# Starting the inverse of the delta stage from 8x8 diagonal blocks solved on VectorE

## What is computed

```
lmat = where(strict, einsum("nbhid,nbhjd->nbhij", kb, kc) * decay, 0.0)
amat = eye + lmat
tinv = triangular_solve(amat, eye, left_side=True, lower=True, unit_diagonal=True)
u = tinv @ (vc * bc[..., None])
w = tinv @ (kb * jnp.exp(gc)[..., None])
```

## Time and profile before

| | |
|---|---|
| median of 3 runs | 877.53 us (875.87 to 878.43) |
| profiled execution | 872.16 us, span 870.3 us |
| mean granted TensorE clock | 0.976 |
| TensorE busy (matmul) | 786.0 us, 90% |
| VectorE, ScalarE, GpSimd busy | 318.2, 169.7, 16.1 us |
| HBM read | 288.30 MB, 334 GB/s over the span |

### The profile page before, as it was taken

The page is one execution under the profiler, slowest core; times in us unless marked ns, Lnnn a source line. Parts: engine busy times, 40 slices in busy tenths (PEclk is TensorE's granted clock), DMA queues, the critical chain, the costliest instruction groups (busy, mean ns, idle before and its releaser), DMA issues.

```text
span 870.3 us, 16568 instructions
## 1 busy us (share of the span) xinstructions
PE 786.0 (90%) x7235; PEld 528.1 (61%) x7235; DVE 318.2 (37%) x662; ACT 169.7 (20%) x327; POOL 16.1 (2%) x21
## 2 busy tenths in 40 slices
PE   4999998989998999999967878999899999988776
PEld 3788667678798655456533443679865556644334
DVE  1154545722523533443322240132453443341324
ACT  3112412213223211111100141040311111110013
POOL 0000000011100000000000000000000000000000
PEclk9999999999999999999989999999999999997899
DMA  9999679383799499999999999993569999999991
GB/s 342 386 358 344 230 236 350 136 306 107 252 390 364 162 393 364 379 414 418 415 416 412 403 386 385 390 411 140 194 233 389 354 396 415 416 418 416 410 398 71
DMA packets 93274, 291.52 MB, mean 335 GB/s; under 512 B 11321, under 2 KB 14479, under 8 KB 78863
## 3 DMA queue, kind: packets, MB, share of 16 engines
q1 hardware_dynamic: 82352, 284.31, 84.2%
q10 hardware_dynamic: 10847, 6.11, 2.4%
HBM read 288.30 MB, written 2.10 MB: 334 GB/s over the span
## 4 chain that ended last, share of the span: by engine, by line
PE 74%; DMA 11%; SPq 9%; DVE 3%; ACT 2%; issue 2%; ACTq 1%; DVEq 0%
PE psum L1322 14%; PE psum L1312 7%; PE psum L1246 7%; PE psum L897 6%; PE psum L1367 6%; DMA scratch<-in_w_exp_up 5%; PE psum L957 5%; PE psum L850 4%; PE psum L1378 4%; PE psum L1488 3%; PE psum L1019 3%; PE psum L1500 3%; SPq L734 3%; DMA ring<-in_w_exp_up 2%; DMA scratch<-in_w_in_odd 2%
## 5 line engine op out<-in xcount | busy, mean ns | idle before, releaser
L1322 PE MATMUL psum<-scratch,hT 128*32 128x512 f32 (+2 forms) x512 | 121.4, 642 | 15.1 <-DMA scratch<-in_w_exp_up 15.1
L1322 PE MATMUL psum<-ring,hT 128*32 128x512 f32 (+1 forms) x416 | 88.2, 621 | 10.8 <-DMA scratch<-in_w_exp_up 10.8
L1312 PE MATMUL psum<-scratch 128*128 128x128 f32 x704 | 82.4, 275 | 0.9 <-DVE scratch L2392 0.9
L1312 PEld LDWEIGHTS psum<-scratch 128*128 128x128 f32 x704 | 80.3, 192 | 1.2 <-issue 1.2
L1322 PEld LDWEIGHTS psum<-scratch,hT 128*32 128x32 f32 (+2 forms) x512 | 35.5, 131 | 64.1 <-issue 64.0
L1322 PEld LDWEIGHTS psum<-ring,hT 128*32 128x32 f32 (+1 forms) x416 | 24.4, 120 | 62.6 <-issue 62.6
L1378 PEld LDWEIGHTS psum<-const,scratch 128*128 128x128 bf16 x480 | 45.1, 97 | 23.8 <-issue 13.6
L897 PE MATMUL psum<-hT,ring 128*128 128x256 f32 x256 | 57.8, 382 | 1.1 <-DVE hT L2012 0.7
L1378 PE MATMUL psum<-const,scratch 128*128 128x256 bf16 x480 | 55.9, 272 | 3.0 <-DVE scratch L2408 3.0
L1246 PE MATMUL psum<-hT,ring 128*128 128x128 f32 x512 | 58.1, 275 | 0.3 <-issue 0.3
L1246 PEld LDWEIGHTS psum<-hT,ring 128*128 128x128 f32 x512 | 57.6, 192 | 0.9 <-issue 0.8
(11 more groups left out here) (316 smaller groups left out, 913.4 us busy)
## 6 DMA issues: line engine op xcount, KB each, us to landing
ring<-in_w_mod SPq DMA_DIRECT2D x42, 1024.0 KB, 8.9
scratch<-in_w_exp_down SPq DMA_DIRECT2D x36, 1024.0 KB, 18.2
scratch<-in_w_exp_gate SPq DMA_DIRECT2D x32, 1024.0 KB, 14.3
scratch<-in_w_exp_up SPq DMA_DIRECT2D x32, 1024.0 KB, 15.8
ring<-in_w_exp_gate SPq DMA_DIRECT2D x24, 1024.0 KB, 11.5
ring<-in_w_exp_up SPq DMA_DIRECT2D x24, 1024.0 KB, 13.6
ring<-in_w_exp_down SPq DMA_DIRECT2D x16, 1024.0 KB, 16.8
ring<-in_w_in_even SPq DMA_DIRECT2D x10, 1024.0 KB, 8.7
```

The source lines that it names most:

```text
L1312: last = mm(bank[b][:, k * P:(k + 1) * P], hrow[:, t, half * 4 + k, :], Pm[:, t, :], start=(t == 0), stop=(t == 1))
L1322: last = mm(bank[0][i * m:(i + 1) * m, :], xg[:, k, i * m:(i + 1) * m], w[e][:, k, :, :], start=(k == 0), stop=(k == KT - 1))
```

## The change

- `delta_rows` cuts L to its 8x8 diagonal blocks, sums each row over the 8 blocks (`cmp8`, 8 numbers per row, since only its own block is not zero), and spreads these over the 8 rows of the block (`blk_D`), instead of making the 2x2 inverse.
- `block_columns(t)`, new on TensorE: one 128x128 by 128x512 product with a mask of ones per 8x8 block, which puts each block's 64 numbers on all of its partitions in bank `t`.
- `eliminate()`, new on VectorE: 7 steps of forward substitution on all 8x8 blocks at once; a step has two products and two differences of 8 to 56 elements per partition. Then two 128x512 products spread the result to `blk_DT`.
- Levels 1 and 2 (of five) are gone: three remain, on blocks of 8, 16 and 32. `delta_inverse0` goes through bank 7 and waits for the modulation M_2, `first_inverse` too.
- The order of TensorE, ScalarE and VectorE around these changes; `("in0", 2)` is now used before `("mod", 1, 0)`, and loads follow in two slots.

```diff
@@ loads
         put("in0", 6)
+        put("in0", 2)
         put_mods(1, 0)
-        put("in0", 2)
@@ block.tensor
+            def block_columns(t):
+
+                pe.wait_ge(S.v_d8, t + 1)
+                mm(bank[t], const[:, C_SAME:C_SAME + P], blk_D[t].rearrange("p d h n -> p (d h n)"), start=True, stop=True).then_inc(S.t_d8, 1)
             def delta_inverse0(t):
 
                 if t == 0:
-                    pe.wait_ge(S.v_gd, 2)
+                    pe.wait_ge(S.v_mod, M_2 + 1)
                 else:
                     pe.wait_ge(S.a_d0, 1)
-                pe.wait_ge(S.v_dt0, t + 1)
+                pe.wait_ge(S.v_d8, NB + t + 1)
...
             rows_to_columns(3, 4)
+            pe.wait_ge(S.v_att, 2)
+            for t in range(NB):
+                block_columns(t)
             pe.wait_ge(S.ld_attn, 32)
             pe.wait_ge(S.a_at, 4)
             rows_to_columns(4, 5)
             mod_turn(M_2)
             pe.wait_ge(S.a_cv, 5)
-            delta_inverse0(0)
-            delta_inverse0(1)
+            tokens_unit(2, 0, 6)
             pe.wait_ge(S.v_att, 4)
+            pe.wait_ge(S.v_d8, 3)
             scores(0)
             scores(1)
-            pe.wait_ge(S.a_d0, 2)
-            tokens_unit(2, 0, 6)
-            mod_chunk(1, 0)
-            pe.wait_ge(S.v_sub, 2)
-            level_left(1)
+            delta_inverse0(0)
             pe.wait_ge(S.a_qkv, 3)
             tokens_unit(2, 1, 6)
-            level_right(1)
+            delta_inverse0(1)
             pe.wait_ge(S.a_silu, 3)
+            pe.wait_ge(S.v_sub, 2)
...
+            pe.wait_ge(S.a_d0, 2)
+            mod_chunk(1, 0)
+            level_left(1)
             mod_chunk(1, 1)
-            level_left(2)
-            mod_chunk(1, 2)
-            level_right(2)
+            level_right(1)
             pe.wait_ge(S.a_at, 7)
             pe.wait_ge(S.v_p, 1)
             transpose_weights(0, 0, 4)
-            level_left(3)
+            mod_chunk(1, 2)
+            level_left(2)
             pe.wait_ge(S.a_at, 8)
             pe.wait_ge(S.a_pt, 1)
             weigh_values(0, 5)
-            level_right(3)
+            level_right(2)
             pe.wait_ge(S.a_qkv, 4)
             mod_chunk(1, 3)
             attention_square(0, 4)
-            level_left(4)
-            mod_turn(M_3)
-            level_right(4)
+            level_left(3)
             pe.wait_ge(S.v_p, 2)
             pe.wait_ge(S.a_ors, 1)
             transpose_weights(1, 0, 4)
             pe.wait_ge(S.v_mixed, 1)
             transpose_weights(1, 1, 5)
-            level_left(5)
+            mod_turn(M_3)
+            level_right(3)
             pe.wait_ge(S.a_pt, 2)
             weigh_values(1, 4)
-            level_right(5)
             attention_square(1, 5)
@@ block.vector
+            def eliminate():
+
+                m8 = psum[:, 0:NB, :].rearrange("p t (d h m n) -> p t d h m n", d=2, h=H, m=SUB)
+                link(V.tensor_copy(inv8.rearrange("p t d h n -> p (t d h) n"), bcast_mid(const[:, C_ROW:C_ROW + SUB], NB * 2 * H)))
+                dve.wait_ge(S.t_d8, 2)
+                for step in range(SUB - 1):
+                    w = SUB - 1 - step
+                    for d in range(2):
+                        i, cs = (step, slice(step + 1, SUB)) if d == 0 else (SUB - 1 - step, slice(0, w))
+                        last = V.tensor_tensor(tmp8[d][:, :, :, 0:w], m8[:, :, d, :, i, cs],
+                                               inv8[:, :, d, :, i].unsqueeze(3).to_broadcast([P, NB, H, w]), ALU.mult)
+                    link(last)
+                    for d in range(2):
+                        cs = slice(step + 1, SUB) if d == 0 else slice(0, w)
+                        last = V.tensor_tensor(inv8[:, :, d, :, cs], inv8[:, :, d, :, cs], tmp8[d][:, :, :, 0:w], ALU.subtract)
+                    link(last)
+                for t in range(NB):
+                    V.tensor_tensor(by_block(blk_DT[t]), inv8[:, t].rearrange("p d h n -> p (d h) n").unsqueeze(2).to_broadcast([P, 2 * H, SUB, SUB]),
+                                    block_mask(), ALU.mult).then_inc(S.v_d8, 1)
@@ delta_rows
-                link(V.tensor_tensor(blk_DT[t], blk_L[t], level(0), ALU.mult))
-                V.tensor_tensor(blk_DT[t].rearrange("p d h n -> p (d h) n"), bcast_mid(const[:, C_EYE:C_EYE + HB], 2 * H),
-                                blk_DT[t].rearrange("p d h n -> p (d h) n"), ALU.subtract).then_inc(S.v_dt0, 1)
+                own = by_block(blk_DT[t])
+                link(V.tensor_tensor(own, by_block(blk_L[t]), block_mask(), ALU.mult))
+                link(V.tensor_reduce(cmp8[t], own.rearrange("p g k n -> p g n k"), AX.X, ALU.add))
+                V.tensor_tensor(by_block(blk_D[t]), cmp8[t].unsqueeze(2).to_broadcast([P, 2 * H, SUB, SUB]),
+                                const[:, C_ROW:C_ROW + SUB].unsqueeze(1).unsqueeze(3).to_broadcast([P, 2 * H, SUB, SUB]), ALU.mult).then_inc(S.v_d8, 1)
...
             delta_rows(1)
+            eliminate()
             modulation(M_2)
@@ block.vector, the levels
             level_values(1)
             level_values(2)
-            level_values(3)
+            attention_out(0, 5)
             modulation(M_3)
-            level_values(4)
             dve.wait_ge(S.v_mod, M_3 + 1)
             gain(2, 1, KT, V_NMIX + KT)
-            attention_out(0, 5)
-            level_values(5)
+            level_values(3)
```

More of the change, by code:

```diff
@@ L49 @@
 LEVELS = 7
+FIRST = 3
+NLEV = LEVELS - 1 - FIRST
+SUB = 8
 RING = 4
@@ L104 @@
 NC_COLS = C_EYE + HB
+C_SAME, C_BLK, C_ROW = C_LEV, C_LEV + 2 * HB, C_LEV + 2 * HB + SUB
 V_BMOD = 0
@@ L127, in shape_constants @@
     rb, qb = r % HB, np.arange(HB)[None, :]
-    for lev in range(LEVELS - 1):
+    for lev in range(FIRST, LEVELS - 1):
         s = 1 << lev
@@ L133, in shape_constants @@
         c[:, o + HB:o + 2 * HB] = same & (qb % (2 * s) < s) & (rb % (2 * s) >= s)
+    c[:, C_SAME:C_SAME + P] = r // SUB == q // SUB
+    c[:, C_BLK:C_BLK + SUB] = rb // SUB == np.arange(SUB)[None, :]
+    c[:, C_ROW:C_ROW + SUB] = r % SUB == np.arange(SUB)[None, :]
     c[:, C_EYE:C_EYE + HB] = rb == qb
@@ L226, in __init__ @@
         self.t_cv = sem("t_cv")
-        self.t_dt = sem("t_dt")
+        self.t_d8 = sem("t_d8")
         self.t_fin = sem("t_fin")
@@ L267, in __init__ @@
         self.v_dd = sem("v_dd")
-        self.v_dt0 = sem("v_dt0")
+        self.v_d8 = sem("v_d8")
         self.v_fin = sem("v_fin")
@@ L516, in build @@
         lamk = small[:, 320:448]
+        cmp8 = [small[:, 192 + 64 * t:256 + 64 * t].rearrange("p (g n) -> p g n", n=SUB) for t in range(NB)]
+        tmp8 = [small[:, 192 + 56 * d:248 + 56 * d].rearrange("p (t h n) -> p t h n", t=NB, h=H) for d in range(2)]
+        inv8 = small[:, 320:448].rearrange("p (t d h n) -> p t d h n", t=NB, d=2, h=H)
         smx = [small[:, 448:456], small[:, 472:480]]
@@ L1033, in delta_inverse0 @@
                             at = (d * H + h) * HB
-                            last = mm(bank[6][r, at:at + HB], blk_DT[t][r, d, h, :], const[r, C_EYE:C_EYE + HB], start=True, stop=True)
-                last.then_inc(S.t_dt, 1)
+                            last = mm(bank[7][r, at:at + HB], blk_DT[t][r, d, h, :], const[r, C_EYE:C_EYE + HB], start=True, stop=True)
+                last.then_inc(S.t_d8, 1)
             def rows_to_columns(n, b):
@@ L1093, in level_right @@
                     pe.wait_ge(S.a_lx, 2 * lev - 1 + t)
-                    if lev < LEVELS - 2:
+                    if lev < NLEV:
                         blocks(bank[2 * t], blk_DT[t], blk_X[t])
@@ L1676, in first_inverse @@
             def first_inverse(t):
-                act.wait_ge(S.t_dt, t + 1)
-                A(blk_D[t].rearrange("p d h n -> p (d h n)"), bank[6], ACT.Copy).then_inc(S.a_d0, 1)
+                act.wait_ge(S.t_d8, NB + t + 1)
+                A(blk_D[t].rearrange("p d h n -> p (d h n)"), bank[7], ACT.Copy).then_inc(S.a_d0, 1)
             def level_copies(lev):
@@ L1745, in _ @@
             columns_copy(4, 5)
+            tokens_copy(2, 0, 6)
             first_inverse(0)
-            first_inverse(1)
             act.wait_ge(S.v_gll, 1)
@@ L1761, in _ @@
                 A(vtok[:, n, :], bank[4 + n], ACT.Copy).then_inc(S.a_at, 1)
-            level_copies(2)
+            level_copies(1)
             act.wait_ge(S.t_pt, 1)
             A(PT[:, 0, :], bank[4], ACT.Copy).then_inc(S.a_pt, 1)
-            level_copies(3)
+            level_copies(2)
             attention_squares(0, 5)
             mod_row(M_3)
-            level_copies(4)
             attention_root(0, 4)
+            level_copies(3)
             act.wait_ge(S.t_pt, 3)
             A(PT[:, :, :], psum[:, 4:6, :], ACT.Copy).then_inc(S.a_pt, 1)
-            level_copies(5)
             attention_squares(1, 4)
@@ L1945, in _ @@
             pool.wait_ge(S.ld_const, 32)
-            for lev in range(1, LEVELS - 1):
+            for lev in range(1, NLEV + 1):
                 for t in range(NB):
```

(10 more changed lines are left out.)

11 lines of the change are left out of this document (5 added, 6 removed).

## The result

The changed kernel takes 868.18 us, median of 9 runs (865.51 to 874.05), against 877.53 (875.63 to 880.61) of 9 runs of the kernel before: a ratio of 0.9905, 95% interval 0.9878 to 0.9933. It is 9.35 us faster, where 14.5 were forecast, and ends 0.18 us above the range. So the gain is about 8 to 14 us and the profile has to say what is missing.

What follows compares the result with a forecast made beforehand. TensorE's order bounds the stretch: 12.0 us of levels + 2.2 of waits - 0.75 = 13.5, 16.1 with the issue stalls gone; 14.5 taken from the 877.53 us median gives 863.0 us, range 858 to 868.

Steps and rivals of the forecast that it cites:

- the one on the stalls: TensorE's issue stalls of 2.0 and 0.6 us before the first `half_rows`: most kept, so 14.5 us gain taken.
- Q: Experiments' theory, not the prediction's: TensorE's instruction fetch queues behind weights already issued, late by what is still to move.
- the wait for the column copies: TensorE's 2.3 us wait for ScalarE, up to 150.94 us: claimed to cover the 2.1 us of `block_columns` products.
- The elimination: `eliminate` on VectorE ahead of the scores: 28 small operations, 4.7 us, hidden with 2.8 us left.
- (a): VectorE's elimination shows ahead of the scores: 0.45 us per operation, 12.6 us, time 868.1 us; chance 0.09.
- (c): Slower: VectorE's elimination operations at 0.8 us or more, `blk_DT[0]` 14.9 us late, more than the gain; chance 0.03.
- The new wait ahead of the last square: TensorE behind `weigh_values(1)`: ScalarE's square with its signals no longer covered by a last level, 0.75 us.
- The two levels: Two full levels of the inverse removed from TensorE, 192 matmul instructions each: 12.0 us saved.
- the waits: TensorE's waits of 0.7 us for the first copied inverse and 1.5 for the first attention output go: 2.2 us.
- The replay: TensorE's order stepped through from 151.9 us: last square ends at 203.6 instead of 220.5 us, 16.9 us gained.
- (d): TensorE's issue stalls go: 860.6 us, inside the forecast's own range; forecast with this case has chance 0.82.
- (b): Experts' weight stream takes the gain back: TensorE waits longer than 25.9 us, time stays at 877.5 us; chance 0.06.

Runs made afterwards that it cites:

- a0_again: The changed kernel, unedited, run again beside other runs of the kernel before: 866.23 against 879.91 us, ratio 0.9859.
- e2: Changed kernel with the second token unit cut in three among the levels and its load moved behind chunk (1, 1): 860.64 against 879.91 us, ratio 0.9785.
- e1: Changed kernel with the weight loads behind chunk (1, 3) held until all three levels' right products are through: 878.8 against 879.91 us, ratio 0.9986.
- e6: The kernel of e2 with the first output weights' load held until the right products of level 2 are through: 863.2 against 878.86 us, ratio 0.982.
- e7: Changed kernel with chunks (1, 3), (1, 6), (1, 7) and first two output weights loaded a megabyte at a time: 862.07 against 877.46 us, ratio 0.9806.
- e8: Changed kernel with the edits of e2 and e7 together: 859.79 us against 877.46 of the kernel before, ratio 0.977.
- e4: Changed kernel with every pair of products in the elimination made three times: 866.87 us against 878.86 of the kernel before, ratio 0.9851.
- e3: Kernel before, with the same loads as in e1 held until its third level's right products are through: 877.68 against 879.91 us, ratio 0.9962.
- e9: Kernel before, with its loads paced in the same way as e7: 877.51 us against 877.46 unpaced, ratio 0.9976.

## Why the prediction missed, step by step

**The step that failed** is the one on the stalls: "Nothing in it takes their cause away, so I keep most of them". It kept 1.6 of 2.6 us (16.1 with all gone, 14.5 taken). They measured 5.8 us, 7.1 in a0_again: a term of the sum mis-sized by 4.2 us, and with the wrong sign, since the stalls took from the gain where 1.0 us had been counted as won. With 5.8 in its place the sum is 13.5 + 2.6 - 5.8 = 10.3, which is what the stretch shows (69.06 - 58.81), and 877.53 - 10.3 = 867.2 stands by the measured 868.18. The prediction had seen that the new order "has a longer stretch of the same, from 170 us", but took the stalls as an amount that stays and not as one that is paid anew for every block of instructions: with both token units ahead of the levels, the fetches of the whole stretch fall among short products, and two stalls become four.

The change also bunched the loads, which the prediction's account of them did not weigh. SyncE issues the six megabytes of chunks (1, 3), (1, 6) and (1, 7) in 10.35 us instead of 17.57, in its timelines of before and of the change:

```profile
166.89 17.57 SPq L687 DMA_DIRECT2D ring<-in_w_mod  x6
171.69 10.35 SPq L697 DMA_DIRECT2D ring<-in_w_mod  x6
```

From 175 to 200 us the mean rate rises from 267 to 326 GB/s and the DMA share from 0.76 to 0.90. How much of the growth comes from the denser products and how much from the bunched loads, no run separates: e2 moves both. That loads in flight are needed for it is shown by e1; that it is the fetch's late start and not its share of bandwidth, by e6 and by the fetch times of e7, and e8 has no stall left. The trace tells when a fetch ran and not when it was asked for, so the queueing itself is inferred from these.

The prediction's words on busy DMA engines in "the second half of the window" are not in the earlier trace rows, which give the mean of 0.53 alone; the 0.76 above bears them out.

The Trainium skill, "Runtime: NRT & Kernel Launch", Instruction fetch mechanics, was weighed there: blocks of 16 KB fetched ahead by the engine's own queue, at a cost that is "mostly hidden". The packets of 16 KB are in the trace, and in e8 all of them are hidden, in e1 all but 1.1 us; under queued weights they cost 5.8 us here. By the Trainium skill's page "DMA: Bandwidth & Descriptors", Queues, rings and completion order, a DMA engine takes turns between queues packet by packet, by which a fetch would not wait for all weights issued; e6, where it ran at the very end of them, doesn't bear that out. In the changed kernel two fetches (178.08 and 184.35) ran in the middle of the stream; Q allows that, for weights issued after the fetch was asked for, but whether it was so is not in the trace.

**What was right.** `block_columns` lies inside the wait for the column copies, of which 0.58 us are left. The elimination takes 4.6 us (4.7 forecast), is hidden by 3.1 us, and e4 shows that margin. Rivals (a) and (c) fall with it: its pairs of products cost 0.25 to 0.34 us. The new wait ahead of the last square is 0.69 us (0.75). The two levels, the waits and that wait are worth 13.5 us in the stretch, as summed, 13.4 by e3 and e1 and 13.1 by e9 and e7. The replay's 16.9 compares a kernel before with its stalls to a change without; that is 69.06 - (58.81 - 5.8) = 16.1, as by terms, so the replay was 0.8 too much. Rival (d), all stalls gone, is not what the change does, but e8 has it, with a stretch 16.1 us shorter than before; that its time is 17.7 us lower is that and the difference between executions.

**What the path to the end did.** All 8.6 us won at `half_rows` reach the experts, as argued against rival (b). Behind them TensorE waits 29.3 us for weights instead of 25.9, and 6.0 us are left. It looks like a part of (b), but differences of this size come without a change: from the first `half_rows` to the end of the span it is 649.8 us in the trace of before, 653.5 and 650.7 in the two of the changed kernel, and 649.5 and 655.1 in the two of e2's; the wait is 28.5 us in e3 and 27.9 in e9, which are the kernel before with its loads moved. So (b) isn't shown, and a part of it isn't excluded: two comparisons of the same two kernels gave medians 9.4 and 13.7 us apart (ratios 0.9905 and 0.9859), and the sum of the terms lies between them. The first expert's load was forecast 15 us earlier and came 7.3 us earlier (217.50 to 210.17): it waits for the products with the values, and these stand behind the stalls.

**The entry.** The changed kernel's profile entered the stretch 1.7 us late, a0_again 0.7 us early, others up to 154.84. The two executions of e2's kernel entered at 150.68 and 154.42: identical code differs here by several microseconds, so this is no effect of the change.

## What to carry to other kernels

An "issue" stall in a run of short matmuls is a cost for each block of instructions, not a fixed amount: before an order is made denser in short instructions, look at what weight loads are queued when its instructions are fetched, and count a possible 1 to 2.7 us for each block. Issue big loads in pieces, each when the one before has landed, in such a stretch: with the same bytes in the same order the stalls fell from 5.8 to 1.5 us in e7. It is no gain where the stalls are short (e9). And holding loads back altogether moves the cost to the small loads that are issued behind the burst, here by ScalarE with 14.6 us of waits.

## What the runs showed of the hardware

- An instruction block is 16 KB on a queue of its own; after a stall TensorE goes on 2.3 to 2.6 us after its transfer begins, in all runs, with idle DMA engines (e6) as with full ones. With nothing else in flight, one block every 4 us feeds 508 matmuls in 18 us without a gap.
- A DMA issue can hold its engine: ScalarE's two issues took 6.90 and 10.26 us at a DMA share of 1.06 (e1), one 7.69 us in e9; others of the same loads took 0.40 and 0.60 us.
- A stall can cost more than itself: after one of 2.68 us in a0_again the following 27 products took 1.75 us, where 1.03 was usual, at a granted clock of 0.50, and after one of 1.86 us in e4 1.54. It doesn't follow each: 13 products took 0.62 us both after 2.35 us of stall in the changed kernel and after 2.07 in a0_again.
- On VectorE a 128x512 reduction over a permuted view took 1.10 us and a copy of 128 elements from a repeated source of 8 took 1.12 us, against 0.69 us for a plain 128x512 operation. Both were hidden here.
- Two executions of one program (e2's) entered this stretch at 150.68 and 154.42 us, with granted clocks of 1.00 and 0.61 in an earlier window (78 to 85 us).
